# Where the weight slots and the streamed tiles begin in SBUF, modulo 128 bytes

## The chip, the core and the metric

The kernel runs on one core of a Trainium2 chip. The metric is the device time of one execution in microseconds; the number given for a kernel is the median of several executions. The profile is one further execution, taken by the hardware profiler.

## The reference, cut to what matters

The program computes four transformer layers, two of each of two kinds, over 512 tokens of width 1024, in float32. Layers of the first kind (`_layer`) project the tokens to 14 groups, run four kinds of attention, gate, project back and normalize:

```
proj = x @ w_in                                     # 1024 -> 3040 columns
ya, yb, yc, ym = banded, latent, windowed, memory attention
y = concat([ya*silu(ag), yb*silu(bg), yc*silu(cg), ym*silu(mg)]) @ w_out
x = layer_norm(alpha * x + y)
```

Layers of the second kind mix half of the width by a two-dimensional Fourier transform and half by windowed attention, and then run a gated feed-forward network of width 2816 with a three-tap convolution:

```
x = x + concat([fourier(u), attention(q, k, v)]) @ w_o
h = conv(rmsnorm(x) @ w_up);  x = x + (silu(gate) * val) @ w_down
```

Nearly all arithmetic is in the dense products with `w_in`, `w_out`, `w_o`, `w_up`, `w_down` and `w_mem_kv`.

## The kernel before, in words

Activations are held transposed: 1024 channels as 8 tiles (`KD`) of 128 partitions by 512 tokens. Every float32 operand of a dense product is split in two parts of type float32r, a rounded one (`_hi`, `_h`) and the rest (`_lo`, `_l`). The function `r3` makes one product of three passes over PE: the low part of the weights with the high part of the tokens, the high with the low, the high with the high. Every pass goes through `mm` (line 573), and so stands in the profile as line L573. A pass loads a 128x128 block of weights into the array (row PEld) and streams a tile of tokens past it (row PE): 512 columns of `xh`/`xl`, `act_h`/`act_l` (inputs of `w_down`) or `mix_h`/`mix_l` (inputs of `w_o`). In some products the roles are turned: in `u_tile` a block of `xh`/`xl` is loaded and 256 columns of `w_hi`/`w_lo` are streamed.

Weights come from HBM in chunks of up to 2064 numbers per partition (`SLOT`), in a fixed order. SP transfers a chunk to `w_stage`, ACT rounds it to `w_hi`, and POOL subtracts to get `w_lo`. Each of the three buffers has two slots; chunk c uses slot c % 2. PE takes a chunk once its `w_lo` is there (`w_split`), 48 passes for a chunk of two 128-column tiles. The order of work is written out by hand, engine by engine, with semaphores between them.

Tiles are placed in SBUF by the helper `place`, which adds each tile's size, rounded up to 32 bytes, to a running offset. Its addresses, in bytes of each partition, come out so: `w_hi` at 16512 and `w_lo` at 49536 (both 0 modulo 128), `xh` at 82432 and `xl` at 98816 (0 modulo 128). A slot is 8256 bytes, so slot 1 of either weight buffer begins at 64 modulo 128. The tiles that share one area, `union`, begin at 64: `act_h`, `act_l`, `mix_h`, `mix_l`, `mem_h`, `mem_l`, `lat_h`, `lat_l`, `u_h`, `u_l`. Blocks within the weight slots, the x, act, mix, mem, lat and u tiles are a multiple of 128 bytes apart, so every pass over those tiles has the phase of its tile; the tables of the Fourier part are 258 numbers wide and have others. Of the passes with 512 columns of `xh` or `xl`, 2040 use slot 0 and 1848 slot 1 by the chunk numbers in the code; of `act` and `mix` half use each. The first chunk of every layer's feed-forward part (number 50 for the first layer) is in slot 0, so its gate and value tiles alternate from there, and so do those of its second half, whose first chunk is number 70. The eight chunks of `w_down` in between are numbers 62 to 69.

Of the kernel before, what the change touches and what calls it, by code (L numbers as in the profile page):

```python
# [17 lines left out]
F32R = mybir.dt.float32r  # L18
I32 = mybir.dt.int32

P = 128
DEPTH = 2
TOK = 512
DM = 1024
KD = DM // P
# [5 lines left out]
BIAS_ROW = 640  # L31
SEQF = 258
SLOT = 2 * 2 * 516
FOLDED = 256
SIN_COLS, EDGE_ROW = 2 * SEQF, 2 * SEQF + 2 * FOLDED
FOLD_COLS = 2 * TOK
# [22 lines left out]
def b2_chunk(l, k):  # L59
    return B2_FIRST + l * B2_CHUNKS + k  # L60


def segments():
# [3 lines left out]
             (b2_chunk(0, 7), "fold", PIECES), (b2_chunk(0, 8), True, PIECES), (b2_chunk(0, 12), None, 0)]  # L67
    segs = [(c, end - c, SLOT, "mixed", c, by_act, pieces) for (c, by_act, pieces), (end, _, _) in zip(marks, marks[1:])]
    for l in range(DEPTH):
        if l:  # L70
            row = b2_chunk(0, 12) + 12 * (l - 1)
            segs.append((b2_chunk(l, 0), 2, SLOT, "mixed", row, True, 1))
            segs.append((b2_chunk(l, 2), 5, SLOT, "mixed", row + 2, True, PIECES))
            segs.append((b2_chunk(l, 7), 1, SLOT, "mixed", row + 7, "fold", PIECES))
            segs.append((b2_chunk(l, 8), 4, SLOT, "mixed", row + 8, True, PIECES))
        c = b2_chunk(l, 12)
# [180 lines left out]
def build(nc, dram, out):  # L257
# [3 lines left out]
    with ctx:  # L261

        base = -(-nc.sbuf_base // 64) * 64
        at = [base]

        def place(name, shape, dt, offset=None):
            size = int(np.prod(shape[1:])) * 4
            where = at[0] if offset is None else offset
            if offset is None:
                at[0] += -(-size // 32) * 32  # L270
            return nc.alloc_sbuf_tensor_at(name, shape, dt, offset=where)

        w_hi = place("w_hi", [P, 2, SLOT], F32R)
        w_stage = place("w_stage", [P, 2, SLOT], F32)
        w_lo = place("w_lo", [P, 2, SLOT], F32R)
        xt = place("xt", [P, KD, TOK], F32)
        xh = place("xh", [P, KD, TOK], F32R)
        xl = place("xl", [P, KD, TOK], F32R)
        g = place("g", [P, KD, TOK], F32)
        probs = place("probs", [P, 3, TOK], F32)  # L280
# [18 lines left out]
        stat = place("stat", [P, 8], F32)  # L299
        rtok = place("rtok", [P, 8], F32)  # L300
        one_row = place("one_row", [P, 2], F32)
        union = at[0]

        km = place("km", [P, 2, MEM], F32, union)
# [257 lines left out]
        def _(pe):  # L562
# [19 lines left out]
            def r3(o, lh, ll, rh, rl, start, stop, last=False):  # L582
                mm(o, ll, rh, start, False)
                mm(o, lh, rl, False, False)
                mm(o, lh, rh, False, stop, last)

            def acquire(name, i=None, per=0):

                v = ring[name][2]
                if v > 0:  # L590
                    pe.wait_ge(freed(name), v if i is None else i * per + v)
                return bank(name)
# [204 lines left out]
            def fourier(l, c0):  # L797
# [14 lines left out]
                def sequence_transform(cs, i, last=True):  # L812

                    pe.wait_ge(S("u_split"), 2 * TT * l + TT * (i + 1))
                    o = acquire(("A", l, cs, i))
                    f = slice(FOLDED * cs + i * P, FOLDED * cs + i * P + P)
                    for t in range(TT):
# [5 lines left out]
                yield  # L823
                f = slice(FOLDED, FOLDED + 1)
                for t in range(TT):
# [10 lines left out]
                for i in range(2):  # L836
                    o = acquire(("pq", l, i))
                    for k in range(2):
                        w = slice(SIN_COLS + k * FOLDED + i * P, SIN_COLS + k * FOLDED + i * P + P)
                        r3(o[:, 0:SEQF], w_hi[:, c % 2, w], w_lo[:, c % 2, w], a_h[:, 2 + k, :], a_l[:, 2 + k, :], k == 0, k == 1, k == 1)  # L840
# [1188 lines left out]
def layouts(i):  # L2029
# [39 lines left out]
    seq = np.concatenate([cosm[:, :SEQF], sinm[:, :SEQF]], 1).astype(np.float32)  # L2069
    mirror = (TOK - np.arange(FOLDED)) % TOK  # L2070
    mirror[0] = FOLDED

# [95 lines left out]
```

## Time and profile before

| | us |
|---|---|
| median of 3 executions | 1707.68 |
| lowest, highest | 1706.57, 1714.58 |
| profiled execution, first to last instruction | 1707.2 |
| PE busy in it | 1661.2 (97%) |
| PEld busy | 1319.1 (77%) |
| DVE, ACT, POOL busy | 788.6, 699.6, 681.4 |

The profile gives no time outside the span; the span lies 0.5 us under the median. A matmul's row has its start and a duration that is longer than its turn on PE, since matmuls are pipelined. How much of PE's time one costs is read from the distance between the starts of two, or from the starts of the first and the last of many.

### The profile page before, as it was taken

What the parts mean: (1) busy time and instruction counts of PE and PEld (TensorE: products, weight loads), DVE (VectorE), ACT (ScalarE), POOL (GpSimd) and SP (SyncE); (2) the same over time, 40 slices, a digit from 0 to 9 for tenths busy, and PEclk for the clock granted to TensorE, in tenths of its full rate; (3) what the DMA queues carried; (4) which work ended last, traced back from release to release, by engine and by line L of the source; (5) the groups of instructions that cost most, each with busy time, mean ns of one, the idle gap of its engine ahead of it and who ended that gap; (6) DMA issues with size and microseconds to landing.
All of it is one profiled execution on the core that took longest, in us unless ns stands there. A gap on an engine that the chain in (4) does not pass through costs nothing.

```text
span 1707.2 us, 23842 instructions
## 1 busy us (share of the span) xinstructions
PE 1661.2 (97%) x8770; PEld 1319.1 (77%) x8770; DVE 788.6 (46%) x1492; ACT 699.6 (41%) x1152; POOL 681.4 (40%) x514
## 2 busy tenths in 40 slices
PE   7999899999989989999999999999999999999999
PEld 6876668787667778778888888887877788888887
DVE  7326664402666267663654035524665454304540
ACT  4445452634545164553443134333564443213331
POOL 3532315443321524535334444345254444444433
PEclk9999999999999989999999999999999999999999
DMA  7222103222210312213222322233221222222222
GB/s 273 100 75 70 57 26 140 83 100 75 71 57 26 112 41 90 76 50 102 96 98 74 102 101 93 72 115 117 74 76 50 99 98 92 77 103 98 98 90 83
DMA packets 26880, 150.69 MB, mean 88 GB/s; under 512 B 3888, under 2 KB 4144, under 8 KB 12912
## 3 DMA queue, kind: packets, MB, share of 16 engines
q1 hardware_dynamic: 23968, 142.78, 24.7%
q10 hardware_dynamic: 2832, 6.84, 1.1%
q8 instruction: 51, 0.84, 0.2%
q14 instruction: 29, 0.24, 0.0%
HBM read 142.66 MB, written 2.10 MB: 85 GB/s over the span
## 4 chain that ended last, share of the span: by engine, by line
PE 90%; DVE 4%; issue 2%; ACT 2%; POOL 1%; DMA 0%; DVEq 0%; POOLq 0%; ACTq 0%
PE ring L573 76%; PE outs L639 3%; PE scores L623 2%; PE ring L623 2%; PE scores L649 2%; PE ring L649 1%; PE ring L663 1%; POOL w_lo L553 1%; DVE tmp L1569 1%; PE ring L697 1%; DVE xt L1770 1%; DVE probs_t L1595 1%; DMA xt<-in_x 0%; DVE qb L1571 0%; ACT xt L1326 0%
## 5 line engine op out<-in xcount | busy, mean ns | idle before, releaser
L553 POOL TENSOR_TENSOR w_lo<-w_stage,w_hi 128x258 fp32r<-128x258 f32 (+6 forms) x478 | 659.0, 1409 | 1005.1 <-ACT w_hi L1105 594.3
L573 PE MATMUL ring<-xh,w_lo 128*128 128x512 f32 x1296 | 517.1, 399 | 16.2 <-DVE w_lo L1527 10.8
L573 PE MATMUL ring<-xh,w_hi 128*128 128x512 f32 x1296 | 511.8, 395 | 0.0
L573 PE MATMUL ring<-xl,w_hi 128*128 128x512 f32 x1296 | 511.3, 395 | 0.0
L573 PEld LDWEIGHTS ring<-xh,w_lo 128*128 128x128 f32 x1296 | 244.8, 189 | 74.6 <-DVE w_lo L1527 10.8
L573 PEld LDWEIGHTS ring<-xh,w_hi 128*128 128x128 f32 x1296 | 244.6, 189 | 55.5
L573 PEld LDWEIGHTS ring<-xl,w_hi 128*128 128x128 f32 x1296 | 245.0, 189 | 53.3
L1458 ACT ACTIVATE w_hi<-w_stage 128x2048 fp32r<-128x2048 f32 (+2 forms) x70 | 116.7, 1667 | 158.2 <-PE ring L573 158.2
L1468 ACT ACTIVATE g<-ring,convw 128x512 f32<-128x512 f32 x88 | 68.2, 779 | 245.3 <-DVE ring L1973 245.3
L1105 ACT ACTIVATE w_hi<-w_stage 128x2064 fp32r<-128x2064 f32 (+2 forms) x85 | 127.7, 1514 | 77.3 <-PE ring L573 67.1
L1955 DVE TENSOR_TENSOR xt<-xt,ring 128x512 f32<-128x512 f32 x48 | 33.0, 688 | 238.2 <-PE ring L573 238.2
L1973 DVE TENSOR_TENSOR ring<-ring,tmp 128x512 f32<-128x512 f32 x88 | 61.2, 699 | 172.1 <-PE ring L573 162.3
L573 PE MATMUL ring<-act_h,w_lo 128*128 128x512 f32 x352 | 139.2, 395 | 0.0
L573 PE MATMUL ring<-act_h,w_hi 128*128 128x512 f32 x352 | 139.0, 395 | 0.0
L573 PE MATMUL ring<-act_l,w_hi 128*128 128x512 f32 x352 | 138.9, 395 | 0.0
L573 PEld LDWEIGHTS ring<-act_h,w_lo 128*128 128x128 f32 x352 | 66.3, 188 | 16.3 <-DVE act_l L1986 0.7
L573 PEld LDWEIGHTS ring<-act_h,w_hi 128*128 128x128 f32 x352 | 66.2, 188 | 15.7
L573 PEld LDWEIGHTS ring<-act_l,w_hi 128*128 128x128 f32 x352 | 66.2, 188 | 15.6
L1154 ACT ACTIVATE probs<-scores,neg_max 128x256 f32<-128x256 f32 (+2 forms) x96 | 50.2, 527 | 62.9 <-DVE neg_max L1612 13.8
L1154 ACT ACTIVATE probs<-ring,neg_max 128x256 f32<-128x256 f32 (+2 forms) x96 | 46.1, 482 | 70.8 <-DVE neg_max L1612 16.5
L1980 DVE SCALAR_TENSOR_TENSOR g<-ring,convw,g 128x511 f32<-128x511 f32 x88 | 66.0, 750 | 12.1 <-DVE g L1978 4.6
L1978 DVE SCALAR_TENSOR_TENSOR g<-ring,convw,g 128x511 f32<-128x511 f32 x88 | 65.2, 741 | 1.0 <-ACT g L1468 1.0
(287 smaller groups left out, 2210.3 us busy)
## 6 DMA issues: line engine op xcount, KB each, us to landing
w_stage<-in_mixed SPq DMA_DIRECT2D x62, 1032.0 KB, 4.8
w_stage<-in_up SPq DMA_DIRECT2D x44, 1024.0 KB, 4.8
w_stage<-in_down SPq DMA_DIRECT2D x16, 768.0 KB, 4.3
w_stage<-in_down SPq DMA_DIRECT2D x16, 640.0 KB, 3.9
xt<-in_x ACTq DMA_DIRECT2D x4, 512.0 KB, 11.4
g<-q SPq DMA_DIRECT2D x16, 128.0 KB, 2.3
out_t<-xt ACTq DMA_DIRECT2D x8, 256.0 KB, 2.0
mem_f<-in_mem SPq DMA_DIRECT2D x1, 1024.0 KB, 9.7
```

The source lines that it names most:

```text
L553: ins = nc.gpsimd.tensor_tensor(w_lo[:, slot, cols], source[:, cols], w_hi[:, slot, cols].bitcast(F32), ALU.subtract)
L573: ins = nc.tensor.matmul(o, lhs, rhs, start=start, stop=stop, skip_group_check=True)
L623: nc.tensor.matmul(acquire(("S", it["n"]))[:, 0:it["nb"] * P], q_of(it), k_of(it, l), start=True, stop=True, skip_group_check=True).then_i ...
L639: ins = nc.tensor.matmul(o_bank[it["o"] % 2][lo:lo + 64, it["qt"] * P:it["qt"] * P + P], v_of(it, l, j), probs_t[:, it["par"], j * P:j * P ...
L649: ins = nc.tensor.transpose(o[:, j * P:j * P + P], probs[:, it["n"] % 3, j * P:j * P + P], ident[:, :])
L1105: ins = A(w_hi[:, c % 2, first:last], source[:, first:last], ACT.Copy)
L1154: A(probs[:, n % 3, 0:w], bank(("S", n))[:, 0:w], ACT.Exp, bias=per_row(neg_max, it), scale=1.0 if it["branch"] == "M" else -1.0, accum_ou ...
L1458: A(w_hi[:, c % 2, 0:width], w_stage[:, c % 2, 0:width], ACT.Copy).then_inc(S("w_hi_done"), 1)
L1468: A(g[:, 4 * s + 2 + v, :], bank((kind, l, f0 + first + s))[:, :], ACT.Identity, bias=convw[:, l, taps, 4 * v + 3:4 * v + 4], scale=convw[ ...
L1973: v.tensor_tensor(bank(name)[:, :], bank(name)[:, :], tmp[:, 0, :], ALU.mult).then_inc(S("normed"), 1)
L1978: step(v.scalar_tensor_tensor(out=cc[:, 1:TOK], in0=hh[:, 0:TOK - 1], scalar=convw[:, l, i * 2 + (f0 + first + s), 4 * c:4 * c + 1], in1=c ...
L1980: v.scalar_tensor_tensor(out=cc[:, 0:TOK - 1], in0=hh[:, 1:TOK], scalar=convw[:, l, i * 2 + (f0 + first + s), 4 * c + 2:4 * c + 3], in1=cc ...
```

## The change: addresses of the tiles

`place` gets an argument `phase`: the running offset is first moved up to that value modulo 128. `w_hi` and `w_lo` are placed at phase 32, `xh` at phase 0, and the shared area `union` at a multiple of 128. Slots stay 8256 bytes (`PITCH = SLOT`).

```diff
+PITCH = SLOT
+LINES = 128
+W_PHASE = 32
...
-        def place(name, shape, dt, offset=None):
+        def place(name, shape, dt, offset=None, phase=None):
             size = int(np.prod(shape[1:])) * 4
+            if phase is not None:
+                at[0] += (phase - at[0]) % LINES
             where = at[0] if offset is None else offset
...
-        w_hi = place("w_hi", [P, 2, SLOT], F32R)
+        w_hi = place("w_hi", [P, 2, PITCH], F32R, phase=W_PHASE)
         w_stage = place("w_stage", [P, 2, SLOT], F32)
-        w_lo = place("w_lo", [P, 2, SLOT], F32R)
+        w_lo = place("w_lo", [P, 2, PITCH], F32R, phase=W_PHASE)
         xt = place("xt", [P, KD, TOK], F32)
-        xh = place("xh", [P, KD, TOK], F32R)
+        xh = place("xh", [P, KD, TOK], F32R, phase=0)
         xl = place("xl", [P, KD, TOK], F32R)
...
         one_row = place("one_row", [P, 2], F32)
+        at[0] += -at[0] % LINES
         union = at[0]
```

No instruction, order, size or wait changes. The addresses modulo 128:

| tile | before | after |
|---|---|---|
| `w_hi`, `w_lo` slot 0 | 0 | 32 |
| `w_hi`, `w_lo` slot 1 | 64 | 96 |
| `w_stage` slot 0, slot 1 | 0, 64 | 32, 96 |
| `xh`, `xl` | 0 | 0 |
| `xt` | 0 | 32 |
| `act_*`, `mix_*`, `mem_*`, `lat_*`, `u_*` | 64 | 0 |
| q, k and v of the first kind of layer | 64 | 0 |
| `q2`, `k2`, `v2`, `w_fold` of the second | 0 | 64 |
| `g`, `probs`, `probs_t`, `tmp`, `ident` | 0 | 0 |

## Rows read from the trace of the kernel before

**Rows 1.** The page's first part: busy time, share of the span, instructions

```profile
span 1707.2 us, 23842 instructions
PE 1661.2 (97%) x8770; PEld 1319.1 (77%) x8770; DVE 788.6 (46%) x1492; ACT 699.6 (41%) x1152; POOL 681.4 (40%) x514
```

**Rows 2.** The chain that ended last: start us, us, what (x matmuls)

```profile
604.45 5.30 POOL w_lo L553 x7
...
632.53 5.68 POOL w_lo L553 x8
...
808.20 343.55 PE ring L573 x1483
...
1153.85 4.67 POOL w_lo L553
...
1292.76 41.96 PE ring L573 x180
...
1353.76 350.30 PE ring L573 x1512
```

**Rows 3.** The page's costliest groups of passes: count, busy us, mean ns

```profile
L573 PE MATMUL ring<-xh,w_lo 128*128 128x512 f32 x1296 | 517.1, 399 | 16.2 <-DVE w_lo L1527 10.8
...
L573 PEld LDWEIGHTS ring<-xh,w_lo 128*128 128x128 f32 x1296 | 244.8, 189 | 74.6 <-DVE w_lo L1527 10.8
...
L573 PE MATMUL ring<-act_h,w_lo 128*128 128x512 f32 x352 | 139.2, 395 | 0.0
```

**Rows 4.** Timeline of PE: start us, us, what; first passes of five chunks

```profile
1057.93 0.39 PE L573 MATMUL ring<-xh,w_lo 128*128 128x512 f32 x1
...
1069.12 0.39 PE L573 MATMUL ring<-xh,w_lo 128*128 128x512 f32 x1
...
1080.11 0.39 PE L573 MATMUL ring<-xh,w_lo 128*128 128x512 f32 x1
...
1091.31 0.39 PE L573 MATMUL ring<-xh,w_lo 128*128 128x512 f32 x1
...
1102.30 0.39 PE L573 MATMUL ring<-act_h,w_lo 128*128 128x512 f32 x1
```

**Rows 5.** Timeline of PE: chunk starts in `w_down`'s first half (36 passes each), then x

```profile
924.42 0.39 PE L573 MATMUL ring<-act_h,w_lo 128*128 128x512 f32 x1
...
932.81 0.39 PE L573 MATMUL ring<-act_h,w_lo 128*128 128x512 f32 x1
...
941.17 0.40 PE L573 MATMUL ring<-act_h,w_lo 128*128 128x512 f32 x1
...
991.45 0.39 PE L573 MATMUL ring<-xh,w_lo 128*128 128x512 f32 x1
...
1002.59 0.39 PE L573 MATMUL ring<-xh,w_lo 128*128 128x512 f32 x1
```

**Rows 6.** Timeline of PE in `u_tile`: slot 1 (661), then slot 0 (675)

```profile
661.13 0.28 PE L573 MATMUL ring<-w_hi,xl 128*128 128x256 f32 x1
...
662.15 0.28 PE L573 MATMUL ring<-w_hi,xl 128*128 128x256 f32 x1
...
675.37 0.29 PE L573 MATMUL ring<-w_hi,xl 128*128 128x256 f32 x1
...
676.44 0.28 PE L573 MATMUL ring<-w_hi,xl 128*128 128x256 f32 x1
```

**Rows 7.** Two chunks, slot 0 and slot 1: busy us by engine, clock, DMA

```profile
core 0: us, PE busy (x) PEld busy (x) DVE busy (x) ACT busy (x) POOL busy (x), PEclk, DMA share, GB/s
1057.90:1069.10 11.20, 11.20 (x49) 9.01 (x48) 5.60 (x8) 4.45 (x5) 4.63 (x1) 1.00 0.28 100
1069.10:1080.09 10.99, 10.99 (x49) 9.01 (x48) 5.60 (x8) 4.45 (x5) 4.62 (x1) 1.00 0.26 89
```

**Rows 8.** Groups of passes in those chunks: slot 0, then slot 1

```profile
L573 PE MATMUL ring<-xh,w_lo 128*128 128x512 f32 x16 | 6.3, 395 | 0.0
...
L573 PE MATMUL ring<-xl,w_hi 128*128 128x512 f32 x16 | 6.3, 392 | 0.0
L573 PE MATMUL ring<-xh,w_lo 128*128 128x512 f32 x16 | 6.2, 388 | 0.0
```

**Rows 9.** Timeline of PE within the slot 0 chunk: four passes in order

```profile
1058.16 0.40 PE L573 MATMUL ring<-xl,w_hi 128*128 128x512 f32 x1
1058.39 0.39 PE L573 MATMUL ring<-xh,w_hi 128*128 128x512 f32 x1
1058.62 0.40 PE L573 MATMUL ring<-xh,w_lo 128*128 128x512 f32 x1
1058.86 0.39 PE L573 MATMUL ring<-xl,w_hi 128*128 128x512 f32 x1
```

## The prediction

> **What bounds the kernel now.** I read the page's busy times first: PE is busy 1661.2 of 1707.2 us, and the next engine, DVE, 788.6 [rows 1]. Since a busy PE need not be a PE at its best, I then read the chain that ended last. It holds two pieces in which PE goes from one L573 pass to the next with nothing between: 343.55 us for 1483 passes and 350.30 us for 1512 [rows 2]. That is 231.7 ns a pass in both. Such passes are most of the work: 3 x 1296 over x, 3 x 352 over act, 3 x 128 over mix, 5328 in all with 512 columns, three equal groups for each tile ([rows 3]: one group each of x and act). 5328 x 231.7 ns is 1234 us, 72% of the span. At 2.4 GHz and one column a cycle a pass would take 213.3 ns; the clock was granted in full there [rows 7], so 18.4 ns a pass, 98 us in all, are lost to something other than the clock. An edit of addresses can only act on that. Loading is not the limit in itself: a block takes 189 ns [rows 3], less than a pass.
>
> **What the trace says of addresses.** Chunks alternate between slot 0 and slot 1, so neighbouring chunks differ in the phase of the weights and in nothing else that PE does. From chunk start to chunk start, 48 passes [rows 4]: slot 0 takes 1069.12 - 1057.93 = 11.19 us and then 11.20, which is 233.2 ns a pass; slot 1 takes 10.99 us twice, 229.0 ns a pass. The other engines do the same work in both, 4.6 us of POOL and 4.45 of ACT in each [rows 7]. The groups say it again: the xh,w_lo pass is 395 ns in slot 0 and 388 in slot 1 [rows 8]. So with the streamed tile at phase 0, weights at 64 are 4.2 ns a pass cheaper than weights at 0.
>
> With the streamed tile at phase 64 no slot is cheap. In `w_down` a chunk is 36 passes: 932.81 - 924.42 = 8.39 us in slot 0, 233.1 ns, and 8.36 in slot 1, 232.2; all 288 take 991.45 - 924.42 = 67.03 us, 232.7 ns [rows 5]; 180 over mix take 41.96 us, 233.1 ns [rows 2]. With 256 columns and turned roles, loaded block at 0: streamed at 64, nine passes take 1.02 us, 113.3 ns; streamed at 0, nine take 1.07 us, 118.9 ns [rows 6]. Three of four comparisons fit "equal phases are dear"; act in slot 0 (64 against 0) is dear without being equal. So phases matter, by 4 to 6 ns a pass, and which rule they follow is open.
>
> **The change part by part.** No instruction, wait or transfer is added, removed or moved; the terms are prices of passes.
>
> 1. x passes in slot 0, weights 0 to 32, stream stays at 0. 2040 passes. Neither 32 nor 96 stands in the trace for a weight block under a 512-column stream, so I bound it: below by the best locked pattern, 113.3 ns for 256 columns, which is 226.6 for 512 if it scales; above by the dearest pattern that holds, 233.3, and for single passes higher still, since starts in slot 0 are now 0.23, now 0.24 us apart (1058.16, .39, .62, .86, [rows 9]); the dear ones are then near 238, as two of them average 233.2 and the cheap one is near 229. The chunk from 991.45 to 1002.59 is at 232.1 [rows 5], so I take 232.8 as the mean of slot 0. I take 229.0, the value of slot 1, because after the change no weight slot has the phase of its stream and the stream is at 0, the two things that the cheap rows have in common. 2040 x 3.8 ns = 7.8 us gained.
> 2. x passes in slot 1, weights 64 to 96: 1848 passes already at 229.0. I take no change. Bounds: 226.6 (4.4 us gained) and 233.2 (7.8 us lost).
> 3. act and mix passes, stream 64 to 0, weights as above. At 229.0: 1056 x 3.7 ns + 384 x 4.1 ns = 3.9 + 1.6 = 5.5 us gained. Bounds: 226.6, some 9 us; nothing gained at 233.
> 4. `u_tile`: stream becomes 32 or 96, loaded block stays at 0. Half of its 384 passes are at 113.3, half at 118.9. All at the low value gives 1.1 us, all at the high one loses as much. I take 0.
> 5. Other tiles that move: `xt`, `w_stage`, q, k, v, `w_fold`. DVE, ACT and POOL are busy 5.6, 4.45 and 4.6 of 11 us in a chunk, and PE hides them [rows 7]. POOL stands on the chain in three places, 5.30 + 5.68 + 4.67 = 15.7 us [rows 2]. No row shows POOL or a transfer at 32; if they were 10% slower or faster it would be 1.6 us either way. I take 0. Where PE was waited for by nothing, a faster PE makes the next chunk due 0.2 us sooner, against over 6 us in which POOL is idle per chunk.
>
> Sum: 7.8 + 5.5 = 13.3 us. 528 of the x passes (eleven tiles by 24 passes by two layers, from the code) are interleaved with attention, where PE also follows DVE's softmax; of the 1.0 us of their slot 0 half I keep half. 12.8 us gained: span 1694.4, and 1695 against the median, which lies 0.5 above the span.
>
> The rows show that which slot the loaded block is in changes the pass by 4.2 ns [rows 4]. The Trainium skill, in "TensorE: Matmul & The Clock Gate", Part 2, says that PE has two independent SBUF read ports, so that loading weights takes no read bandwidth from the running matmul; by it alone the two slots would cost the same and the change nothing. The measurement decides here: the slots differ. The same page gives N / 2.4 GHz + 2.5 ns for back-to-back passes, 215.8 ns at 512 columns; no row here comes near that, and going there would be an estimated 5328 x 15.9 ns = 85 us, which I do not expect.
>
> **The rivals.**
>
> A, nothing to measure: 1706. 32 and 96 lie between 0 and 64; if the price of a pass varies evenly between equal (233.2) and opposite (229.0) phases, every pass costs 231.1, and 5328 x (231.7 - 231.1) is 3 us, of which act and mix give most. Or the unit that matters is longer than 128 bytes, and new pairs fall as the old did, some cheap, some dear. For it: act in slot 0 contradicts the simple rule. Against it: the same place at 0/64 is sharply better and repeats in every chunk. The skill's "SBUF — State Buffer", section "Door 1: The DMA port swizzle", gives lines of 16 bytes; all phases here are multiples of 32, so by that page nothing would change either. The alternation of slots [rows 4] speaks against a unit that small.
>
> B, slower: 1717. The mechanism is a block read that begins at 32 or 96, in the middle of a 64-byte unit, and meets the stream in one more unit than a block at 0 or 64. Place: every 512-column pass; it shows first in slot 1. Price: the x passes of slot 1 go from 229.0 to 233.2 (+7.8 us), act and mix stay, slot 0 stays, `u_tile` loses 1.1: +9 us. If each pass costs one 238 ns step more often it goes to 1725 and above, with all at 238 to 1741. It decides from 1.6 ns a pass in the mean upwards (8.5 us / 5328). For it: no cheap row has a start off 64. Against: nothing in the trace shows such a cost.
>
> C, much faster: 1681. All passes lock in the pattern that `u_tile` has in slot 1, 113.3 and 226.6 ns: 5328 x 5.1 ns = 27 us, a little less where attention is interleaved, 26. For it: that pattern exists and is perfectly even. Against: in 512-column passes only one group of slot 1 comes near it, xh,w_lo, with 388 ns where its neighbours have 392 [rows 8].
>
> **How the numbers follow.** A measurement of this kernel tells 0.5%, 8.5 us, from no change: faster is under 1699.1, slower over 1716.2. Forecast (both slots as slot 1 now) 0.36; C 0.13; A 0.28; B 0.23, of which a part ends just under the bound and is offset by cases of the forecast that do worse in one slot only. That gives faster 0.48, same 0.30, slower 0.22. The range leaves out the deeper half of C and the tail of B: 1681 to 1718; the likeliest case alone has 1690 to 1700.
>
> **What would show it right or wrong.** In the feed-forward loops, chunk starts 10.99 us apart in both slots, where 11.19 and 10.99 alternate now; the group xh,w_lo at 388 to 392 ns in all chunks of those loops; the act part of 288 passes at 66.0 us where it is 67.03; the two long pieces of the chain at 229 ns a pass. Step 1 fails if slot 0 stays above 231; step 2 if slot 1 rises above 230; step 3 if act keeps 232.7 with its stream at 0, in which case another unit than 128 bytes sets the price. Step 5 fails if POOL's 4.6 us a chunk change. The whole is wrong if the mean pass stays within 1.6 ns of 231.7.

## The result and the profile after

The change makes the kernel slower. Median 1720.47 us (1716.44 to 1726.74, 6 runs) against 1708.24 us (1706.57 to 1714.58, 6 runs) of the kernel before, run beside it: ratio 1.0075 with a 95% interval of 1.0054 to 1.0097. I had forecast 1695 us and a gain.

The first part of the page of the kernel after, busy time, share of the span and instructions:

```profile
span 1714.6 us, 23842 instructions
PE 1667.0 (97%) x8770; PEld 1315.2 (77%) x8770; DVE 788.7 (46%) x1492; ACT 699.2 (41%) x1152; POOL 681.0 (40%) x514
```

PE is busy longer, 1667.0 us after 1661.2, and PEld 3.9 us less; the other engines stay within 0.5 us [rows 1]. The chain that ended last has the same long pieces (start us, us, what):

```profile
809.64 346.60 PE ring L579 x1483
...
1158.33 4.67 POOL w_lo L559
...
1358.12 353.35 PE ring L579 x1512
```

346.60 us for 1483 passes is 233.7 ns a pass, and 353.35 for 1512 the same, where both were 231.7 [rows 2]. 5328 passes x 2.0 ns = 11 us, which is the difference of the medians (12.2 us) within its interval (9 to 17 us). The spans of the two profiled executions differ by 7.4 us only, and the granted clock has a part in that. The execution before had a stretch at half the clock (0.50, 1.2 GHz) at its 180th microsecond, in which it lost 3.0 us to the other (us, busy by engine, clock, DMA):

```profile
179.90:186.70 6.80, 6.80 (x27) 4.29 (x26) 1.59 (x7) 1.81 (x6) 0.00 (x0) 0.50 0.14 58
```

The execution after had none there, but one of 3.4 us at 427 us, which cost it 1.5 us. At one and the same mean granted clock the kernels are some 10 us apart: at 0.989 the kernel after took 1716.4 us twice, the kernel before 1705.0 to 1707.5 us in nine executions.

Which passes became dearer is read from the first passes of successive chunks, on PE's timeline (start us, us, what); chunks of slot 0 and slot 1 alternate:

```profile
1061.79 0.39 PE L579 MATMUL ring<-xh,w_lo 128*128 128x512 f32 x1
...
1072.98 0.39 PE L579 MATMUL ring<-xh,w_lo 128*128 128x512 f32 x1
...
1084.22 0.39 PE L579 MATMUL ring<-xh,w_lo 128*128 128x512 f32 x1
...
1095.41 0.39 PE L579 MATMUL ring<-xh,w_lo 128*128 128x512 f32 x1
...
1106.65 0.39 PE L579 MATMUL ring<-act_h,w_lo 128*128 128x512 f32 x1
```

Slot 0 takes 11.19 us for 48 passes, 233.1 ns, as before; slot 1 takes 11.24, 234.2 ns, where it took 10.99, 229.0 ns [rows 4]. The cheap slot is gone and the dear one did not become cheap. The clock was granted in full, and the other engines are as busy as they were [rows 7], by the view of the two chunks (us, busy by engine, clock, DMA):

```profile
1061.76:1072.95 11.19, 11.19 (x49) 9.02 (x48) 5.60 (x8) 4.45 (x5) 4.62 (x1) 1.00 0.25 87
1072.95:1084.19 11.24, 11.24 (x49) 9.03 (x48) 5.60 (x8) 4.46 (x5) 4.62 (x1) 1.00 0.28 100
```

The page's groups of passes (count, busy us, mean ns of one) agree: x from 399 to 402 ns, act from 395 to 396 [rows 3].

```profile
L579 PE MATMUL ring<-xh,w_lo 128*128 128x512 f32 x1296 | 521.0, 402 | 17.1 <-DVE w_lo L1533 10.6
...
L579 PE MATMUL ring<-act_h,w_lo 128*128 128x512 f32 x352 | 139.2, 396 | 0.0
```

A group's mean includes the pipelined tail of a pass, some 162 ns more than the interval between starts: 389 stands for 226.7, 396 for some 233.4. "ns a pass" below is always the interval between starts.

### The profile page after: what moved, and what is told of

The parts are those of the page before. It is cut to its first block, busy times and chain, and to the rows that moved or that the text cites. A ratio compares the mean times of both kernels' runs of the same rounds, so it can differ in the third digit from the quotient of the medians.

```text
span 1714.6 us, 23842 instructions
## 1 busy us (share of the span) xinstructions
PE 1667.0 (97%) x8770; PEld 1315.2 (77%) x8770; DVE 788.7 (46%) x1492; ACT 699.2 (41%) x1152; POOL 681.0 (40%) x514
## 4 chain that ended last, share of the span: by engine, by line
PE 75%; issue 12%; POOL 7%; DVE 3%; ACT 2%; DMA 1%; ACTq 0%; POOLq 0%; DVEq 0%
PE ring L579 66%; POOL w_lo L559 7%; PE outs L645 2%; PE scores L629 1%; PE ring L629 1%; PE ring L703 1%; PE scores L655 1%; PE ring L655 1%; PE ring L669 1%; DMA xt<-in_x 1%; POOL w_fold L548 1%; ACT w_hi L1111 1%; DVE tmp L1575 0%; ACT xt L1332 0%; ACT xh L1334 0%
```

## The experiments

Three theories were on record before the first of them. U: a block that starts off a 64-byte unit costs in itself, rival B of the prediction. L: only the addresses of the pair modulo 256 or more matter, and before had one lucky pair. X: the other engines' accesses to SBUF make the difference. A fourth, R, was written down after e1 and comes from its map: the price depends on the start of the loaded block minus that of the stream, modulo 256. It is L made exact.

**e1_map, the disputed price alone.** A kernel that only streams: 48 passes of 512 columns for each pair of start addresses, nothing else running; the layers are left out. `w` and `x` are the byte starts of block and stream.

```diff
+            F.append((lambda o, w, x, **k: nc.tensor.matmul(o, w, x, **k), dict(w=0, x=0)))
+            F.append((lambda o, w, x, **k: nc.tensor.matmul(o, w, x, **k), dict(w=32, x=0)))
...
+            F.append((lambda o, w, x, **k: nc.tensor.matmul(o, w, x, **k), dict(w=224, x=192)))
...
+                wo, xo = c["w"] // 4, c["x"] // 4
...
+                            at = wo + k * step + (r % 2) * 128 * (step > 0)
+                            xat = xo + x + k * 512
+                            wa, xa = w[:, at:at + m], x_all[:, xat:xat + n]
```

> Passes of the same kind as the kernel's (float32r, 128x128 block, 512 columns, low-high, high-low, high-high over eight k), 48 for each pair of start addresses, with nothing else running. It leaves the layers out and times only PE. Theory U (a weight block that begins off a 64-byte unit is read with one unit more and costs about 4 ns a pass, whatever the stream): weights at 32, 96, 160, 224 give 233 to 234 ns between starts for every stream phase; weights at 64 or 192 with the stream at 0 give 229.0. Theory L (only the address modulo 256 or more of the pair matters, and before had one lucky pair): weights at 192 with the stream at 0 give 229, weights at 64 with the stream at 0 or at 128 do not. Theory X (the other engines' accesses to SBUF make the difference): with nothing else running all pairs cost the same. A block of 32 columns instead of 128 tells whether the length of the load matters: under U it costs at least 3 ns less than 128 columns where these are dear.

Groups by pair; the line number tells it: L51 to L58 have the stream at 0 and the weights at 0, 32, 64, ... 224; L60 is weights 32, stream 32; L69 64 and 64; L87 128 and 128.

```profile
L51 PE MATMUL ring<-x,w_hi 128*128 128x512 f32 x32 | 9.9, 389 | 0.0
L52 PE MATMUL ring<-x,w_hi 128*128 128x512 f32 x32 | 10.1, 395 | 0.0
L53 PE MATMUL ring<-x,w_hi 128*128 128x512 f32 x32 | 10.1, 396 | 0.0
L54 PE MATMUL ring<-x,w_hi 128*128 128x512 f32 x32 | 10.1, 396 | 0.0
L55 PE MATMUL ring<-x,w_hi 128*128 128x512 f32 x32 | 10.0, 395 | 0.0
L56 PE MATMUL ring<-x,w_hi 128*128 128x512 f32 x32 | 10.0, 393 | 0.0
L57 PE MATMUL ring<-x,w_hi 128*128 128x512 f32 x32 | 10.0, 393 | 0.0
L58 PE MATMUL ring<-x,w_hi 128*128 128x512 f32 x32 | 10.0, 395 | 0.0
L60 PE MATMUL ring<-x,w_hi 128*128 128x512 f32 x32 | 9.9, 390 | 0.0
...
L69 PE MATMUL ring<-x,w_hi 128*128 128x512 f32 x32 | 9.8, 389 | 0.0
...
L87 PE MATMUL ring<-x,w_hi 128*128 128x512 f32 x32 | 9.9, 389 | 0.0
```

The mean intervals of the same passes, from the differences of successive starts:

| block start - stream start, mod 256 | 0 | 32 | 64 | 96 | 128 | 160 | 192 | 224 |
|---|---|---|---|---|---|---|---|---|
| ns a pass | 226.7 | 233.4 | 233.4 | 234.4 | 232.4 | 233.4 | 228.8 | 233.3 |

The row holds within 0.6 ns for streams at 0, 32, 64, 96, 128 and 192: where all passes have one difference, only the difference counts, and equal addresses are the cheapest of all. X falls, since the prices differ with nothing else running. U falls too: it wanted 233 to 234 ns for a block at 32 whatever the stream, and with the stream at 32 that block is at 227; and it wanted blocks of 32 columns at least 3 ns cheaper where 128 are dear, but at 160 and 224 they cost 233.3 and 233.4. Before, the pairs were x 128 and 192 (measured 233.2 and 229.0), act 64 and 128 (233.1 and 232.2). After, `xh` lies at 128 modulo 256 and the weights at 160 and 224, so x has 32 and 96, act 160 and 224: all four are in the dear part. The 128-byte view of the prediction did not see that `xh` moved as well.

**e2_w64_both**: weights at 64 modulo 128 in both slots, longer slots.

```diff
-PITCH = SLOT
+PITCH = SLOT + 16
-W_PHASE = 32
+W_PHASE = 64
```

> Both weight slots at 64 modulo 128 (a slot is 64 bytes longer), all streamed tiles at 0. Theory U (weights off 64 bytes are dear, weights at 64 under a stream at 0 are cheap): x, act and mix passes at 229.0 ns in both slots, 1694 to 1697 us. Theory L (the phase modulo 256 counts; here x is at 128 and the weights at 192 and 64 modulo 256): passes stay at 232 to 234 ns, 1708 to 1718 us.

1713.27 us (10 runs), ratio 1.0018, 1.0001 to 1.0035. U's gain of 11 us and more isn't there; L's 1708 to 1718 us came. Since `w_hi` and `w_lo` now lie 128 apart modulo 256, each chunk mixes differences 64 and 192; its long piece of chain is 301.44 us for 1299 passes, 232.05 ns, between the two prices of the map.

The single slots show a limit of R. In act chunks of slot 0 and in x chunks of slot 1 the passes with `w_lo` have difference 64 and the two with `w_hi` 192, so R's mean is (233.4 + 2 x 228.8) / 3 = 230.3 ns for both. The starts of one act chunk (36 passes) and of one x chunk (48):

```profile
927.15 0.40 PE L579 MATMUL ring<-act_h,w_lo 128*128 128x512 f32 x1
...
935.40 0.40 PE L579 MATMUL ring<-act_h,w_lo 128*128 128x512 f32 x1
...
1004.65 0.39 PE L579 MATMUL ring<-xh,w_lo 128*128 128x512 f32 x1
...
1015.85 0.39 PE L579 MATMUL ring<-xh,w_lo 128*128 128x512 f32 x1
```

That is 229.2 ns in the act chunk and 233.3 in the x chunk. The differences are the same and the prices are not, so the difference alone is not enough where it alternates from pass to pass. What else counts there is open.

**e3_w32_only**: the change's shift of the weights alone, x and act where they were before.

```diff
-LINES = 128
-W_PHASE = 32
+LINES = 256
+W_PHASE = 160
-        at[0] += -at[0] % LINES
+        at[0] += (64 - at[0]) % LINES
```

> Only the weights move, to 32 and 96; x stays at 0 modulo 256 and act, mix at 64 as before. Theory U: x passes at 233 to 234 in both slots, the slower time of the change comes back, 1716 to 1720 us. Theory L (x went from 0 to 128 modulo 256 in the change, and that cost it): x passes of slot 1 stay near 229 or fall elsewhere, 1700 to 1710 us.

1720.20 us (4 runs), ratio 1.0057, 1.0040 to 1.0075. The chain's piece is 346.34 us for 1483 passes, 233.5 ns. L's guess that the move of x alone had cost the time, with slot 1 near 229, falls: slot 1 is at 233.4. R, with differences 160 and 224, and U both fit.

**e4_union_only**: the other half, `union` at 128 modulo 256, weights where they were.

```diff
-W_PHASE = 32
+W_PHASE = 0
```

> Only the shared area moves, from 64 to 0 modulo 128, so that act and mix stream from 0; the weights stay at 0 and 64 and x at 0. If the stream's own phase made act dear in slot 1 (my prediction's step 3): act passes of slot 1 fall from 232.2 to 229.0, those of slot 0 stay at 233, 2 to 3 us gained, 1705 us. Theory L: act stays at 232 to 234 in both slots, 1707 to 1709 us.

1706.68 us (10 runs), ratio 0.9986, 0.9968 to 1.0004. The chunk starts in `w_down` (36 passes each, slot 0 first):

```profile
924.33 0.39 PE L579 MATMUL ring<-act_h,w_lo 128*128 128x512 f32 x1
...
932.52 0.40 PE L579 MATMUL ring<-act_h,w_lo 128*128 128x512 f32 x1
...
940.91 0.39 PE L579 MATMUL ring<-act_h,w_lo 128*128 128x512 f32 x1
```

8.19 us in slot 0 is 227.5 ns, where it was 233.1; 8.39 in slot 1 is 233.1, where it was 232.2 [rows 5]. By R these are the differences 0 and 64. My step 3 had it the other way round: by its rule slot 0, with equal phases, is the dear one. L, which wanted 232 to 234 in both slots, failed in slot 0 as well. Over half of 1440 passes -5.6 ns and over half +0.9 make -3.4 us; the median moved by -2.4 us (interval -5.5 to +0.7), which is too small to show by itself.

**e5_all_0_mod_256**: both weight slots and all streamed tiles of x, act and mix at 0 modulo 256; the small tiles go into the gaps between the slots.

```diff
-PITCH = SLOT
-LINES = 128
-W_PHASE = 32
+PITCH = SLOT + 48
+LINES = 256
+W_PHASE = 0
...
+        at[0] -= (PITCH - SLOT) * 4
+        row_inv = place("row_inv", [P, 2, 8], F32)
+        sink_exp = place("sink_exp", [P, 8], F32)
...
```

> Both weight slots and all streamed tiles at 0 modulo 256 (a slot is 192 bytes longer; a few small tiles fill the gaps). Theory R (the price of a pass follows the start of the block minus the start of the stream, modulo 256, as in the map: 0 gives 226.7 ns, 32 and 64 233.4, 96 234.4, 128 232.4, 160 233.4, 192 228.8, 224 233.3): all 512-column passes at 226.7 to 227.5 ns where they run unbroken, 5328 x 4.6 ns = 24 us less than before, 1682 to 1688 us. Theory U (64-byte units) and my prediction's rule (equal phases are dear): 233 ns, 1716 us.

1703.27 us (12 runs), ratio 0.9967, 0.9952 to 0.9982. The passes do what R says: the chain has 288.56 us for 1272 of them, 226.9 ns. At the forecast 1682 to 1688 it did not arrive. Most of what was missing goes back to one small instruction. POOL and DVE in e5 (start us, us, what):

```profile
695.55 5.58 POOL L550 TENSOR_TENSOR w_fold<-w_stage 128x256 f32<-128x256 f32 x8
```

```profile
695.95 5.20 DVE L1644 TENSOR_TENSOR row_sum<-row_sum,sink_exp 128x8 f32<-128x8 f32 x1
```

and the same two before:

```profile
700.12 5.56 POOL L542 TENSOR_TENSOR w_fold<-w_stage 128x256 f32<-128x256 f32 x8
```

```profile
700.56 0.32 DVE L1636 TENSOR_TENSOR row_sum<-row_sum,sink_exp 128x8 f32<-128x8 f32 x1
```

An addition of 8 elements a partition, begun 0.4 us into POOL's run of eight instructions (four additions, four subtractions), lasts 5.20 us instead of 0.32 and ends with POOL's run. It does so in both layers of this kind, and the attention behind it, which waits for `row_sum`, ends some 5.4 us later each time.

The wait costs more than itself. PE stands still for 3.35 us, and at 701.40, near the end of that, its granted clock falls to 0.50 for 6.80 us, in which PE is busy for 6.46 (first PE's row after the wait, then two stretches: us, busy by engine, clock, DMA):

```profile
701.74 1.98 PE L631 MATMUL scores<-k,q 64*128 64x384 f32 x4 [3.35 <-DVE probs_t L1603]
```

```profile
694.60:701.40 6.80, 3.80 (x38) 3.23 (x34) 6.69 (x8) 2.09 (x8) 6.53 (x10) 1.00 0.45 155
701.40:708.20 6.80, 6.46 (x37) 5.05 (x38) 3.48 (x10) 2.65 (x6) 0.00 (x0) 0.50 0.01 4
```

The same follows at 1244 us, and e8 below repeats both. Against e9, which doesn't have this wait, e5 loses 6.8 us in the first of these layers and 7.4 in the second, 5.4 and 5.3 of them at the wait and the rest some 30 to 50 us later, where e5 has two stretches of 3.4 us at 0.50 and e9 has one. The mean granted clock of the twelve executions of e5 is 0.978 to 0.984, that of e9 0.987 to 0.991.

**e6_change_stream_160**: the changed kernel's weights at 32 and 96 stay, the streams move to 160 modulo 256, so that the differences are 0 and 64.

```diff
-LINES = 128
-W_PHASE = 32
+LINES = 256
+W_PHASE = 160
-        xh = place("xh", [P, KD, TOK], F32R, phase=0)
+        xh = place("xh", [P, KD, TOK], F32R, phase=W_PHASE)
-        at[0] += -at[0] % LINES
+        at[0] += (W_PHASE - at[0]) % LINES
```

> The changed kernel with its weights at 32 and 96 modulo 128 left where they are; x, act, mix and the rest of the shared area move by 32 or 160 bytes, to 160 modulo 256, the phase of slot 0. Theory R: slot 0 at 226.7 ns (difference 0), slot 1 at 233.4 (difference 64); against before that is about 8 us less, 1699 to 1702 us, and 18 less than the change. Theory U (a block off a 64-byte unit costs by itself): no better than the change, 1716 us or more.

1703.56 us (12 runs), ratio 0.9963, 0.9945 to 0.9981. It is 1.6 us above R's forecast. The chain's 293.01 us for 1272 passes are 230.4 ns, slot 0 at 227.3 and slot 1 at 233.3. With the weight addresses of a slower kernel this one is faster than before: U, and with it rival B as it was told, falls in the whole kernel too. A start off a 64-byte unit costs nothing in itself.

**e7_map_fine**: the map again, over other distances and sizes (`n` columns streamed, `m` columns loaded), with the layers left out.

```diff
+            F.append((lambda o, w, x, **k: nc.tensor.matmul(o, w, x, **k), dict(w=8, x=0)))
...
+            F.append((lambda o, w, x, **k: nc.tensor.matmul(o, w, x, **k), dict(w=0, x=0, n=256)))
...
+            F.append((lambda o, w, x, **k: nc.tensor.matmul(o, w, x, **k), dict(w=96, x=0, m=1)))
```

> Passes only, nothing else running, stream at 0, the layers left out. Theory R: blocks 256, 512 and 768 bytes on cost as at 0 (226.7), 320 and 576 as at 64 (233.4); blocks 8 to 24 bytes on stay near 226.7 if the unit is 32 bytes. If the stall comes from the volume of the load, blocks of 64, 32 or 1 columns cost no more than 227 at a difference of 96, against 234.4 for 128; if it comes from where load and stream start, they stay near 233. With 256 columns difference 0 is cheapest too (113.3) if the rule is the same for them; roles turned, 64 gave 113.3 before, and 0 is open.

Weights at 0, 256 and 320 (L51, L59, L60), then blocks of 64 columns at differences 0 and 96 (L80, L81), and of one column at the same two (L84, L85):

```profile
L51 PE MATMUL ring<-x,w_hi 128*128 128x512 f32 x32 | 9.9, 389 | 0.0
...
L59 PE MATMUL ring<-x,w_hi 128*128 128x512 f32 x32 | 9.9, 389 | 0.0
L60 PE MATMUL ring<-x,w_hi 128*128 128x512 f32 x32 | 10.1, 395 | 0.0
...
L80 PE MATMUL ring<-x,w_hi 128*64 128x512 f32 x32 | 9.9, 391 | 0.0
L81 PE MATMUL ring<-x,w_hi 128*64 128x512 f32 x32 | 9.8, 389 | 0.0
...
L84 PE MATMUL ring<-x,w_hi 128*1 128x512 f32 x32 | 10.0, 394 | 0.0
L85 PE MATMUL ring<-x,w_hi 128*1 128x512 f32 x32 | 10.0, 394 | 0.0
```

The period is 256 bytes: 256, 512 and 768 are at 226.7 ns, 320 and 576 at 233.4. The forecast for narrower blocks failed both ways. One column has 231.7 ns at either difference, dearer than a full block at 0 and cheaper than one at 96; 32 columns have 231.7 and 230.6; and with 64 columns the order is turned round, 230.0 at difference 0 and 226.6 at 96. So the price doesn't grow with the volume of the load, and R holds for blocks of 128 columns, not for narrower ones. With 384 columns both 0 and 96 have 173.3 ns. With 256 columns streamed difference 0 is no longer the cheapest, against the forecast: 120.0 and 119.8 at 0 and 160, 117.3 to 118.6 at the rest. The 256-column pair (192, turned roles) had 113.3 in one map and 117.8 in the other, and so had starts below 32 bytes two values (16: 226.7 and 233.3); for these the passes just before seem to matter, and R isn't claimed for them.

**e8_all_0_repacked**: e5 with `row_sum` and `sink_exp` put back among the other small tiles, to see if their place made the addition slow.

```diff
-        row_inv = place("row_inv", [P, 2, 8], F32)
-        sink_exp = place("sink_exp", [P, 8], F32)
+        neg_max = place("neg_max", [P, 2, 8], F32)
+        row_inv = place("row_inv", [P, 2, 8], F32)
```

> As the kernel with all phases at 0 modulo 256, but row_sum and sink_exp, which it had moved beside the weight buffers, back among the small tiles; other small tiles fill the gaps. There the DVE addition row_sum<-row_sum,sink_exp took 5.2 us twice, at 696 and 1239 us, where before takes 0.32, and the attention behind it was 5.5 us late each time. If the addresses of these tiles did that, both are near 0.3 us again and the time falls by about 10 us, to 1693. If it is the moment at which the addition meets POOL's eight back-to-back pieces of w_fold, the moments are as in the kernel it is made from and both stay at 5.2 us, 1703 us.

1703.19 us (12 runs), ratio 0.9959, 0.9943 to 0.9975; the addition takes 5.18 us again, twice. It isn't the address of these tiles.

**e9_all_0_sink_columns**: e8 with the addition as eight additions of one column, each with a scalar operand.

```diff
-step(v.tensor_tensor(sums, sums, sink_exp[:, :], ALU.add))
+for c in range(8):
+    ins = v.tensor_scalar(row_sum[:, it["o"] % 2, c:c + 1], row_sum[:, it["o"] % 2, c:c + 1], sink_exp[:, c:c + 1], None, ALU.add)
+step(ins)
```

> The same, and that addition is written as eight one-column additions, each with one SBUF tensor and a per-partition scalar instead of two SBUF tensors. If the two-tensor form must wait for POOL, no piece of it takes over 0.3 us and the sum of eight is under 1 us: about 10 us less than with 5.2 us twice, 1693 us. If POOL's run blocks any DVE instruction at that moment, one of the eight takes about 5 us, 1703 us.

1689.00 us (1684.61 to 1690.92, 5 runs), ratio 0.9878, 0.9856 to 0.9901: the fastest of all, 1.2% under the kernel before and 4 us under the forecast of 1693. Page, groups of passes, and the eight columns under the same eight pieces of POOL:

```profile
span 1682.8 us, 23926 instructions
PE 1632.8 (97%) x8770; PEld 1313.2 (78%) x8770; DVE 796.9 (47%) x1576; ACT 699.5 (42%) x1152; POOL 685.4 (41%) x514
...
L581 PE MATMUL ring<-xh,w_lo 128*128 128x512 f32 x1296 | 513.6, 396 | 17.2 <-DVE w_lo L1535 10.8
L581 PE MATMUL ring<-act_h,w_lo 128*128 128x512 f32 x352 | 137.2, 390 | 0.2
```

```profile
692.48 5.65 POOL L550 TENSOR_TENSOR w_fold<-w_stage 128x256 f32<-128x256 f32 x8
```

```profile
692.90 1.06 DVE L1645 TENSOR_SCALAR row_sum<-row_sum,sink_exp 128x1 f32<-128x1 f32 x8
```

DVE is busy 8.3 us more than before, PE 28.4 us less. The eight columns take 1.06 us with POOL in its run, 0.20 us each.

The span falls by 1707.2 - 1682.8 = 24.4 us, and 5328 passes x 4.6 ns would be 24.5, but that they agree is luck. The execution before had two stretches of 6.8 us at half the clock, at 180 and 477 us, that this one has not, and each is worth 3.0 us of the 24.4. The medians differ by 20.6 us, and at a mean granted clock of 0.989 e9 took 1687.8 us against 1705.0 to 1707.5: some 18 us. That is three quarters of 24.5. The rest is missing outside the feed-forward parts: between the 190th and the 475th microsecond of the kernel before stand 744 of the passes, and e9 gains 0.6 us there, where the 3471 passes from 760 to 1165 and from 1300 on give 15.2 us. In e9 POOL's `w_lo` holds 10.5% of the chain that ended last, against 0.9% before: there the passes wait for chunks, and a cheaper pass is no time gained.

**e10_before_sink_columns**: that edit alone, on the kernel before.

```diff
-step(v.tensor_tensor(sums, sums, sink_exp[:, :], ALU.add))
+for c in range(8):
...
```

> The kernel before with its addresses, and only the addition of the sinks written as eight one-column additions. In before that addition takes 0.16 to 0.63 us, so there is no long wait to remove: no change within 2 us of 1709 if the addresses made the gain of the last experiment, and the wait was only a by-product of where the faster passes put that addition. If the eight additions by themselves bring it, 1689 to 1698 us.

1710.15 us (12 runs), ratio 1.0004, 0.9984 to 1.0025: nothing. The gain of e9 is that of the addresses, and the columns only keep it from being given back.

**e11_all_at_96**: e9 with the streams at 160 modulo 256 and the weights at 0, so that every difference is 96 in both slots, the price of the changed kernel's slot 1.

```diff
-        xh = place("xh", [P, KD, TOK], F32R, phase=0)
+        xh = place("xh", [P, KD, TOK], F32R, phase=160)
-        at[0] += -at[0] % LINES
+        at[0] += (160 - at[0]) % LINES
```

> The fastest kernel so far with one thing doubled back: the streamed tiles move from 0 to 160 modulo 256 and the weights stay at 0, so that block minus stream is 96 for every 512-column pass, the dearest value of the map. No weight begins off a 256-byte line. Theory R: 234.4 ns a pass in place of 226.7, 5328 x 7.7 ns = 41 us at most, less where attention covers it: 1722 to 1730 us, slower than the kernel before. Theory U (only a block that begins off 64 bytes is dear): 1689 us as with all at 0.

1726.79 us (4 runs), ratio 1.0116, 1.0082 to 1.0150, as R forecast. Its chain:

```profile
815.24 347.60 PE ring L581 x1483
...
1303.28 42.17 PE ring L581 x180
...
1364.69 354.40 PE ring L581 x1512
```

234.3 to 234.4 ns a pass in all three, over x, act and mix. e9 and e11 have the same weight addresses and the same instructions, and differ in where the streams begin, and with them the tiles that are placed behind them: 226.9 against 234.4 ns, 1689.00 against 1726.79 us.

## Why the prediction was wrong

**Where to look was right.** The prices of the 5328 passes decide: the order of the layouts follows from them, apart from the 14 us that one DVE addition took back in e5 and e8, and the other engines' work in a chunk stayed within 0.01 us.

**Step 1 failed**, by its own test (slot 0 above 231). It priced x in slot 0 at 229.0 because "no weight slot has the phase of its stream and the stream is at 0". It measured 233.1, so the 7.8 us were not gained. The failure is the rule: I took equal phases to be dear from differences that were equal modulo 128 only. Modulo 256 no pair before was equal, and the pair that I called equal was 128 apart. e1, e4 and e5 show that truly equal starts are the cheapest of the map, 226.7.

**Step 2 failed.** Slot 1 was to stay at 229.0. Its difference went from 192, the second cheapest of the map, to 96, the dearest: 234.2, 1848 x 5.2 ns = 9.6 us lost, more than the bound of 7.8 that I gave. The reason is that I had the upper bound from the dearest row before (233.2), and a dearer pattern existed.

**Step 3 failed.** act and mix were to fall to 229.0; they stand at 233.3 (8.40 us for 36 passes), 0.6 ns above their 232.7. The prediction had named what this would mean, that "another unit than 128 bytes sets the price", and e7 shows the unit. Step 1's and step 3's -13.3 us thus became about +1, and step 2's 0 became +9.6; together the 11 us above.

**The sum took a pass's price for time** in all but half of 1.0 us. e9 shows that only some three quarters of it arrive, so even with the right prices the forecast gain would have come out smaller.

**Step 4 held.** The 256-column groups of `u_tile` did not move. Before and after, the largest of them:

```profile
L573 PE MATMUL ring<-w_hi,xl 128*128 128x256 f32 x128 | 37.3, 291 | 0.0
```

```profile
L579 PE MATMUL ring<-w_hi,xl 128*128 128x256 f32 x128 | 37.4, 292 | 0.0
```

**Step 5 held**: POOL is busy 4.62 us in each chunk and stands on the chain with 4.67 us at the same place, as before [rows 2, 7].

**The rivals.** B named the side, the first place (slot 1) and nearly the size, 1717, but its mechanism is refuted: e6 keeps starts at 32 and 96 and is faster than before. That its number came near was luck. A's second half, that the unit is longer than 128 bytes and "new pairs fall as the old did", was the right mechanism; but I had given it a time of 1706, as if the new pairs had to average what the old did, and they are all in the dear part. C's end, all passes at 226.6, exists and e9 reaches it, at 1689 and not 1681: those passes don't need the change but its opposite, equal starts. Its estimate of 26 us was too large; the medians give 20.6, and part of that is clock.

What could have been seen blind: the addresses modulo 256 stood in the code. The four rows of before (x 128: 233.2, x 192: 229.0, act 64: 233.1, act 128: 232.2) fit "difference modulo 256" without a contradiction, while by the 128-byte rule act in slot 0 was an exception, which I counted as three of four. They would not have given the prices of 32, 96, 160 and 224; but seeing that all four new differences were unmeasured takes the ground from a forecast of 229.0, and leaves about 227 to 234 with the most known pairs dear.

On the two read ports that the Trainium skill gives PE ("TensorE: Matmul & The Clock Gate", Part 2): from them the page concludes that a load takes no SBUF read bandwidth from the running matmul, and by that alone the addresses would make no difference, but with the same loads and the streams at other starts e9 and e11 are 7.5 ns a pass apart. Whether it is read bandwidth that is lost there isn't shown.

## What to carry over

Where TensorE is busy nearly all the time with float32r passes of 512 columns and blocks of 128, give the loaded block and the stream the same start address modulo 256 bytes, in every buffer slot; the length of a slot then has to be a multiple of 256 bytes. When an exception remains to a rule of phases, try a longer period before pricing anything with it. And when a faster engine's gain doesn't arrive, look for a short instruction that has become long: here the moved meeting of two engines took back 14 of 21 us, part of them through a stretch at half the clock that followed each wait. Compare single executions only with their granted clocks beside them: two stretches of 6.8 us at half the clock made a gain of 18 us look like 24.

## What the runs showed of the hardware

- The price of a 512-column float32r pass over a block of 128 columns runs from 226.7 to 234.4 ns with the difference of two SBUF start addresses modulo 256 bytes, where all passes have the same difference. Where two differences alternate (e2), or the block has 64 columns or fewer (e7), this rule isn't enough. Why, and why the best is 17/16 of 213.3 ns at the full clock, stays open; I have shown the rule and not its mechanism.
- Loading one column instead of 128 in the shadow of a pass saves nothing against a full aligned block (231.7 ns against 226.7), and 2.7 ns against the dearest one (234.4).
- After PE had stood still for 3.35 us in e5, its granted clock was 0.50 for 6.80 us; the same in the second such layer and in e8, and not in e9, where that wait is missing.
- A DVE addition of two SBUF tiles of 8 columns, begun 0.4 us into a run of eight POOL instructions, took 5.2 us, twice in an execution, in e5 and e8; one-column additions with a scalar operand took 0.20 us in the same place. The Trainium skill, "SBUF — State Buffer", section "SBUF: two separate sides", tells of a port pair that DVE and GpSimd share under an exclusive lock held for a whole instruction, and of a DVE instruction with two SBUF inputs as one that needs it against a GpSimd instruction that reads SBUF. The traces agree with a lock that is given up only at an instruction's end: in the eight traces of kernels with this addition, twelve of the additions take 0.27 to 0.32 us and end 0.02 to 0.03 us after the first of POOL's eight instructions, and the four of 5.2 us end as long after the last. These four had begun 0.40 to 0.44 us into the run and the twelve 0.44 to 0.49. Why the wait was then for all eight and not for one or two is open.
